# Seven block products for pairs of delta-rule projections, in a four-layer hybrid backbone

## The reference

```python
def streams(h):                     # h: tokens x 1024
    p = h @ w_in                    # q, k: 8 heads x 128; v, z: 16 heads x 128; 64 gate columns
    qkv = silu(centred_dwconv(p[..., :GDN_CONV_DIM], conv_w))     # 4 taps over the tokens
    z = p[..., GDN_CONV_DIM:GDN_CONV_DIM + GDN_VAL_DIM]
    ...                             # q and k to unit length, decays from the gate columns
```

## Time and profile before

| | |
|---|---|
| median of three runs | 3240.86 us |
| the profiled execution: span from first to last instruction | 3251.1 us |
| TensorE busy | 3092.5 us (95%) |
| VectorE, ScalarE, GpSimd busy | 53%, 47%, 27% |
| mean granted clock of TensorE | 0.978 |
| DMA | 261.93 MB, mean 81 GB/s |

### The profile page before, as it was taken

How to read it: one execution, slowest core, us unless ns; L and a number is a source line. 1 busy time by engine, 2 the same in 40 slices (tenths; PEclk the granted TensorE clock), 3 DMA queues, 4 the chain that set the end, 5 groups by cost and what they waited for, 6 DMA issues and landing times. The chain is left out here.

```text
span 3251.1 us, 55663 instructions
## 1 busy us (share of the span) xinstructions
PE 3092.5 (95%) x21673; PEld 2016.4 (62%) x21673; DVE 1731.2 (53%) x3543; ACT 1539.1 (47%) x3296; POOL 873.2 (27%) x652
## 2 busy tenths in 40 slices
PE   5889999999999999999999999897999999999998
PEld 3357777777777764455445555444777777777753
DVE  1156666666666652244443334346676767776632
ACT  3155555555555531256432444335655565555521
POOL 0044434533533410011001101003544435343400
PEclk9699999999999999999999999898999999999999
DMA  9921111211211126022311111102212222121135
GB/s 375 330 68 54 56 56 55 67 56 45 72 56 51 45 89 235 1 68 64 128 33 31 29 46 52 72 4 80 66 53 69 59 60 63 57 68 53 43 120 192
DMA packets 224097, 261.93 MB, mean 81 GB/s; under 512 B 19418, under 2 KB 158948, under 8 KB 223716
## 3 DMA queue, kind: packets, MB, share of 16 engines
q1 hardware_dynamic: 223844, 258.46, 24.7%
HBM read 239.15 MB, written 19.27 MB: 79 GB/s over the span
## 5 line engine op out<-in xcount | busy, mean ns | idle before, releaser
L898 PE MATMUL ps<-hT,W 128*128 128x512 f32 (+1 forms) x2656 | 1001.2, 506 | 3.0 <-DVEq L192 2.0
L898 PEld LDWEIGHTS ps<-hT,W 128*128 128x128 f32 x2656 | 470.5, 193 | 195.1 <-issue 165.6
L1331 DVE CAST_PREDICATED arena<-mask,ps 128x384 bf16<-128x384 uint32 x448 | 253.2, 565 | 223.2 <-PE ps L967 174.3
L1148 ACT CAST arena<-ps 128x384 bf16<-128x384 f32 x384 | 166.9, 482 | 347.7 <-PE ps L954 346.7
L2372 PE MATMUL ps<-arena 128*128 128x512 f32 x712 | 311.2, 595 | 2.3 <-SPq L192 2.0
L1333 DVE CAST_PREDICATED arena<-mask,ps 128x384 bf16<-128x384 uint32 x448 | 250.9, 560 | 0.0
L2372 PEld LDWEIGHTS ps<-arena 128*128 128x128 f32 x712 | 134.5, 191 | 167.1 <-issue 162.8
L2007 PE MATMUL ps<-hT,W 128*128 128x512 f32 (+1 forms) x608 | 218.2, 493 | 0.6 <-DMA W<-in_att_w_in 0.4
L1455 POOL TENSOR_TENSOR arena<-arena 128x768 f32<-128x768 f32 (+1 forms) x32 | 44.4, 1389 | 636.0 <-ACT arena L1192 636.0
L1268 DVE SCALAR_TENSOR_TENSOR arena<-arena,vec 128x770 f32<-128x770 f32 (+1 forms) x192 | 205.4, 1070 | 6.8
L967 PEld LDWEIGHTS ps<-arena 128*128 128x128 bf16 x2304 | 144.7, 98 | 55.4 <-issue 51.0
(11 more groups left out here) (284 smaller groups left out, 6177.0 us busy)
## 6 DMA issues: line engine op xcount, KB each, us to landing
arena<-in_ada_w SPq DMA_DIRECT2D x24, 2048.0 KB, 19.5
W<-in_gdn_w_in SPq DMA_DIRECT2D x95, 512.0 KB, 4.0
arena<-decay_sums SPq DMA_DIRECT2D x64, 384.0 KB, 4.1
W<-decay_rows SPq DMA_DIRECT2D x64, 384.0 KB, 5.0
arena<-in_gdn_w_out SPq DMA_DIRECT2D x32, 512.0 KB, 10.5
W<-in_gdn_w_out SPq DMA_DIRECT2D x30, 512.0 KB, 3.4
arena<-gated SPq DMA_DIRECT2D x32, 384.0 KB, 7.7
gated<-arena SPq DMA_DIRECT2D x24, 384.0 KB, 2.3
```

Of the source, the lines that this page charges most:

```text
L898: mm = pe.matmul(ps[:, b, 0:t1 - t0], w[:, i, :], env.hT[:, i, t0:t1], start=(i == 0), stop=(i == KD - 1))
L1148: act.copy(half_cols(Xb[d], s, d), ps[:, 2 * d, 0:384].rearrange("p (c b s) -> p c b s", c=NT, s=s)).then_inc(*inxe.up(m, lv, d))
L1331: dve.copy_predicated(half_cols(Mb[d], s, d), wide(env.m4[:, d, lv]), src_m).then_inc(*inm.up(m, lv, d, "m"))
```

## The change

The projections of k with q, and of v with z, are formed as a 2 x 2 block product: the two tiles are the two block rows, the contraction is halved (4 matmuls in place of 8), and the tokens are halved (384 each in layer 0, 256 each in layer 3, there of the latent tokens alone). Seven products named 1 to 7 take the place of eight. A1 .. A7 are those of k and q (once per two slots), B1 .. B7 those of v and z (every slot). The first pair of each kind keeps the old form, so that 7 A pairs and 15 B pairs of each layer are changed. In layer 3 the context columns of k and v stay separate (c0, c1).

Some products accumulate on another one that stays in the bank (`CHAIN`) and that ScalarE has copied out meanwhile. All products are copied out by ScalarE, and VectorE adds the parts one position later (`late`). Sums of activations go into the space of `env.x` (GpSimd, once per layer), so x is loaded again from DRAM at the end of slot 14; after layer 2 it is stored for this. The sums of the weights are formed on GpSimd for k and q (`a_sums`, `a_last`) and on VectorE for v and z (`b_sums`, `b_last`). The constants for rotary attention leave the start's load and are loaded ahead of layer 2.

```diff
+CHAIN = {"A6": "A1", "A3": "A5", "A4": "A7", "B6": "B1", "B5": "B6", "B3": "B5", "B4": "B7"}
+def slot_order(n, last):
...
+    elif odd:
+        order = ["A7"] * heads + (["c1"] * fresh if last else o[:1]) + ["A4"] * heads + ["B1"] * fresh + (o if last else o[1:])
+        order += ["B6", "B2", "B5", ("B7", 0, 1), "B3"] * fresh
+    else:
+        if last:
+            order = ["c0", "A5", "A2", "A3"] * heads + o + ["B1", "c1", "B6", "B2", "B5", ("B7", 0, 1), "B3"] * fresh
+        else:
+            order = ["A5", "A2", "A3"] * heads + o[:1] + ["B1"] * fresh + o[1:] + ["B6", "B2", "B5", ("B7", 0, 1), "B3"] * fresh
...
+    spare = [("B7", i, i + 1) for i in range(1, KD2)] * fresh + [("B4", i, i + 1) for i in range(KD2)] * fresh
+    if odd and n + 1 < 2 * GH - 2:
+        spare += [(use, i, i + 1) for use in ("A1", "A6") for i in range(KD2)]
...
+        def strassen(n, use, i, o):
...
+            elif i == 0 and which != 2:
+                form = {6: 2, 5: 1, 3: 4, 7: 3, 4: 3}[which]
+                sig, key = (aform, h) if kind == "A" else (bform, m)
+                pe.wait_ge(sig.sem, sig.at(key, form))
...
+            return pe.matmul(o, w, x, start=(i == 0 and use not in CHAIN), stop=(i == KD2 - 1), ...)
...
-                if p == 14 and m in U:
+                if p == (15 if n >= 0 else 14) and m in U:
                     silu_v(m)
+                if p == 15 and n in U and n:
+                    gates(n)
                 for use in done[n, p] if n > -2 or p >= 2 else []:
                     keep(n, use)
...
                 if p == 7 and n in TILES and n > -2:
-                    conv_x(n)
+                    conv_x(n, True, False)
+                if p == 8 and n in TILES and n > -2:
+                    conv_x(n, False)
...
-                if p == 13 and m in U:
+                if m in U and p == (14 if n >= 0 and step_at(n, "B3") == 13 else 13):
...
+                    conv(1, 16 + m, convv, m, 0, True, p == 14)
...
+                if m in U and m and p == min(3, max(0, first_step(n, "B6") - 2)):
+                    b_sums(m)
+                for key in late[n, p]:
+                    add(*key)
+                    if key[1] == "B2":
+                        b_last(m)
...
+        def a_last(h):
+            kb = env.W[:, 0, KD2:]
+            pool.wait_ge(ad.sem, ad.at(2 * h - 2, "A2"))
+            pool.wait_ge(aform.sem, aform.at(h, 2))
+            pool.tensor_tensor(kb, kb, SUMS["A"][1], ALU.subtract).then_inc(*aform.up(h, 4))
```

More of the change, by code:

```diff
@@ L160, in build @@
         env.ps = ctx.enter_context(nc.psum_tensor("ps", [P, 8, 512], F32))
[L161 to L164, removed]
+        env.ident, env.ones, env.cap_f, env.cap_b, env.perm = (env.cst[:, i * P:(i + 1) * P] for i in range(5))
         env.m4 = env.mask[:].rearrange("p (two l c) -> p two l c", two=2, l=LEVELS)
@@ L547, in fill_plan @@
 def fill_plan(last):
     plan, done, uses, before, last_in = {}, {}, [], {}, {}
-    bank = 6
     for n in range(-2, GU + 1):
-        unit, tile = 0 <= n + 1 < GU, n < 2 * GH - 2
-        fresh = unit and n >= 0
         short = last and n % 2 == 1
[L559 to L587, removed]
-            else:
[L589 to L602, removed]
@@ new lines, in fill_plan, with cost, begin @@
+        order, small, spare = slot_order(n, last)
+        bank, spare_bank, doing = 6, None, None
+        spent, goal, turn = 0.0, 0.0, 0
+        def cost(use):
+            if use[0] in "AB":
+                return (1.0 if last else 1.5,) * KD2
+            return COST[use[0]] if use[0] in COST else COST[use[1]] if use[0] in "XVZ" else ((1,), (2,))[int(use[1])]
+        def begin(use, of_spare):
+            nonlocal bank, spare_bank
+            if use in CHAIN and (n, CHAIN[use]) in before:
+                at = before[n, CHAIN[use]][0]
+            elif of_spare and spare_bank is not None:
+                at = spare_bank
+            elif not of_spare and spare_bank is not None and spare:
+                at = 13 - spare_bank
+            else:
+                at = bank
+            if of_spare:
+                spare_bank = at
+            before[n, use] = (at, last_in.get(at))
+            last_in[at] = (n, use)
+            bank = 13 - at
@@ L603, in fill_plan @@
+        step_of = lambda item: (item[0], item[1], True) if isinstance(item, tuple) else (item, CT if item == "G0" and short else 0, False)
+        total = sum(sum(cost(step_of(i)[0])) if not isinstance(i, tuple) else cost(i[0])[0] for i in order + small + spare if step_of(i)[0][0] != "t")
+        share = max((total - sum(FILL[:2])) / sum(FILL[2:]), 0.5) + 0.001
+        least = (lambda use: FIRST[use]) if n == -2 else (lambda use: AFTER.get(use[0], 0))
         for p in range(POS):
@@ L606, in fill_plan @@
             here = []
[L607 to L611, removed]
+            while spent < goal or n == -2:
+                if doing is None:
+                    if order:
+                        queue = order
+                    elif small and p >= least(small[0]) and (turn == 0 or not spare):
+                        queue = small
+                    elif spare:
+                        queue = spare
+                    else:
+                        break
+                    use, step, single = step_of(queue[0])
+                    if p < least(use):
+                        break
+                    queue.pop(0)
+                    turn = 1 if queue is small else 0
+                    if step == 0 or not single:
+                        begin(use, single)
+                    doing = [use, step, step + 1 if single else len(cost(use))]
+                use, step, stop = doing
+                here.append((use, step, len(cost(use))))
+                spent += cost(use)[step]
+                doing = [use, step + 1, stop] if step + 1 < stop else None
             plan[n, p] = here
@@ L614, in fill_plan @@
             uses += [(n, use) for use in done[n, p]]
-        assert at == len(steps)
+        assert not order + small + spare and doing is None
     return plan, done, uses, before
@@ L1193, in silu_x, with gates @@
                                ACT.Silu).then_inc(*sx.up(n, i))
-            if n == -1 or last and n > -2:
+            if n > -2:
+                hold(env, act)
+                act.preload_act_table_set(LNEXP)
+        def gates(m):
+            act.wait_ge(dev.sem, dev.at(m - 1, "B4"))
+            sz = v.sz[:, m % 2, LO:T]
+            act.activation(sz, sz, ACT.Silu).then_inc(*zsd.up(m))
+            if m == GU - 1:
                 hold(env, act)
@@ L1264, in conv @@
             lo = lo + 2 if lo else 0
[L1265 to L1266 removed]
+            if first:
+                dve.tensor_scalar(acc[:, lo:CONVW], pad[:, lo:CONVW], col(0), None, ALU.mult).then_inc(*sig.up(key, 0))
+            for w in range(1 if first else 2, 4 if second else 2):
                 dve.wait_ge(sig.sem, sig.at(key, w - 1))
@@ L1463, in gpsimd @@
             m = n + 1
+            if n in TILES and n >= 0 and n % 2 == 0:
+                a_last((n + 2) // 2)
             if m in U:
@@ L2336, in out_phase @@
     stored = seq("stored", per(1) if last else [], 16)
+    before_last = l == DEPTH - 2
+    kept = seq("x_kept", [(n,) for n in range(SEQ // P)] if before_last else [], 16)
     def sync(sp):
```

247 lines of the change are left out of this document (212 added, 35 removed).

## The result

The changed kernel takes 3510.1 us (median of 4 runs, 3497.8 to 3516.0), the kernel before on the same chip 3241.5: ratio 1.081, 95% interval 1.079 to 1.084, **268.6 us slower** by the medians, 264 by the ratio. Forecast were 3312 us and +71. The direction was right; the size lies far outside the range of 3210 to 3355.

What follows compares the result with a forecast made beforehand. TensorE's program order was taken as the clock in both layers. Saving -93, waits +175, VectorE +5, convolution split -14 and start -2 summed to +71 us: 3312 us on the median, range 3210 to 3355.

Steps and rivals of the forecast that it cites:

- The saving, -93 us: TensorE's matmul stream: 2.6 us saved a pair in layer 0, 1.65 in layer 3, for 22 pairs each.
- Rival 4: Nothing is multiplied less: a 384-column matmul costs nearly what 512 do; 3444 us, chance 0.02.
- ScalarE's hand-overs and `a_last`: TensorE's waits for bank copies, the norm and GpSimd's subtraction: 76 us in layer 0, 99 in layer 3, together +175.
- Touching products: Successive uses of one bank with nothing between: TensorE waits 0.75 us in layer 0, 0.65 in layer 3.
- B3 at p 9: Layer 3, odd slots: B3 waits 2.7 us for B5's copy, behind `silu_x` and two table loads on ScalarE.
- G1 at p 15: Layer 3, odd slots: G1 directly behind A6 waits 3.3 us for ScalarE's cast, table load, silu, gates and copies.
- G1's and k0's waits in layer 0: Odd slots, positions 15 and 16: G1 waits 0.65 us and k0 1.0 us for copies queued on ScalarE.
- rivals 1 and 2: Smaller waits: 1, only short hand-overs, 3178 us, chance 0.12; 2, waits 90 to 125 us, about 3244 us, 0.15.
- VectorE, 5 us: Added weight sums and additions, +6.1 us a slot in layer 0, +5.0 in layer 3, mostly hidden: 5 us in all.
- Rival 3: VectorE becomes the bound where its share passes 75%, in the inverse's loop: +40 on the forecast, 3350 us, chance 0.16.
- Splitting the convolution (-14): Both convolutions split over two positions, removing most of layer 3's waits behind masked copies: 1 us a slot, -14.
- What would show it: Right: waits for ScalarE's copies, slots of 64 and 60 us. Wrong: layer 0 slots under 62.5 us, or VectorE-ended waits.

Runs made afterwards that it cites:

- x1: Changed kernel with ScalarE's evictions of finished products placed ahead of silu_x, silu_v and the gates in their position, nothing left out: 3508.6 us, ratio 1.080.
- y1: Changed kernel with VectorE's weight sums and late additions and GpSimd's splitting all cut to one column: 3384.9 us, ratio 1.043.
- z2: Kernel before with four added 512-column VectorE additions a slot on scratch memory, three at position 8 and one at 9: 3272.4 us, ratio 1.009.
- y2: Kernel before with four added 512-column VectorE additions a slot on scratch memory, three at position 3 and one at 9: 3320.3 us, ratio 1.022.
- z3: y2 with the four added additions cut to one column each: 3247.0 us, ratio 1.000 to the kernel before.
- y3: y1 with the edit of x1 (evictions ahead of Silu in ScalarE's position): 3373.6 us, ratio 1.039.

## Why the prediction was wrong

**The saving, -93 us: right.** Six records of 384 columns in the changed kernel's layer 0 are one row:

```profile
632.03 2.10 PE L972 MATMUL ps<-hT,W 128*128 128x384 f32 x6
```

Less the last record's own 0.49 us, its five spacings are 0.322 us each, as drawn between the two ends of the earlier trace rows. Rival 4 is out. (By the prediction's own terms layer 3 saves 17.2 - 15.5 = 1.7 us a pair, not 1.65; that makes 1 us.)

**ScalarE's hand-overs and `a_last`: right in place and nearly in size.** A4 behind A7: 1.8 forecast, 2.1 in the list (line 1221). `a_last`: 1.4 against 1.5, 14 times, 21.2 us in all (the operation itself took 1.27 us, not the 1.17 of the earlier trace rows; twice VectorE's 0.685 would be 1.37, where the prediction wrote 1.34). A1 behind B4: 1.75 against 1.5. Touching products: 0.75 against 0.57 in the list and 0.84 in the start times. Layer 3, B3 at p 9: 2.7 against 3.0; G1 at p 15: 3.3 against 2.9; G0 behind the norm: 1.65 against 2.1. Not found were G1's and k0's waits in layer 0. Over two slots 10.85 against 8.0, and 14.15 against 12.0; by 7 that is 140 us for the 175 forecast, so rivals 1 and 2, with waits under 104 and of 90 to 125 us, are out as well. x1 adds that these waits aren't independent of the loop: two of them could be removed for nothing. No run takes the hand-overs away as a whole; their price rests on the lists.

**VectorE, 5 us: the step that failed.** The text counted its instructions (+6.1 and +5.0 us a slot; the terms that it names make 5.8 in layer 0) at durations from rows in which nothing ran beside them, and took the added work as lying in idle time. The lists show 12.0 and 5.6 us of waits for VectorE in two slots beyond the norm's, after 0 and 1.6: by 7 some 112 us. y1 has 126 for VectorE and its neighbour together, clock included: the time lost to the half clock is 122.0 us in the changed kernel, 82.5 in y1 and 72.8 in the kernel before, and that TensorE's fewer waits brought it down is likely, not shown. Two errors lie in the step. First, the sums were put at position 3, in the middle of the 17 us block in which GpSimd splits and caps. The kernel before has that block too, and a sign of the price was in its trace, which I had read past. Beside the 1021 ns for 770 columns of the earlier trace rows stood (2300 to 3050 us):

```profile
L1268 DVE SCALAR_TENSOR_TENSOR arena<-arena,vec 128x512 f32<-128x512 f32 x21 | 24.4, 1161 | 0.7
```

The shorter shape is the slower one: in one slot its four instructions run from 2583.10 us, and GpSimd's capping from 2582.07 to 2585.84. A mean that doesn't grow with the size is a wait inside the instruction. Second, even 2.8 us without a neighbour cost a microsecond a slot (z2): at that place the loop had less room than the "idle gaps" suggest.

The Trainium skill states the rule in SBUF — State Buffer, section "SBUF: two separate sides": a VectorE instruction with two inputs in SBUF, or in a mode that uses both of its ports, and one of GpSimd share a pair of ports under an exclusive lock held for a whole instruction, and the loser blocks. The runs agree: 0.146 us becomes 1.59. In the traces VectorE's operations with an operand in PSUM stay at 0.95 us for 768 columns throughout, as the earlier trace rows' 284 ns for 128 columns do. Which of the two cases holds for the convolution's first instruction no run shows; it reads one tensor and one column of constants, and is held as well (1.42 us at 646.79, with GpSimd's line 1663 until 647.80, against 0.61 alone). I had weighed another rule of the skill, on GpSimd's speed, and not this one, which speaks against the change.

**Rival 3** (VectorE becomes the bound above 75%, 3350 us, chance 0.16) named the right engine. Its busy share did come to 75 and 77%. But the share isn't what decides: y2 has the loss of 73 us with VectorE at 69% in the stretch of layer 0, and z3 none.

**Not in the sum at all.** The account of two slots of layer 0 is 124.5 - 7.8 (saving) + 20.0 - 0.8 (waits listed) = 135.9, measured 143.4; in layer 3, 111.7 - 4.95 + 17.6 - 1.6 = 122.8, measured 131.2. 7.5 and 8.4 us are open, about 111 us in all. A part is the clock. In every second slot of layer 0 there is one stretch of 6.83 us at the lower level. It is the second of these lines, between the time before and after it (columns as in the earlier trace rows; the granted clock is the third number from the end):

```profile
560.30:567.10 6.80, 4.47 (x39) 2.87 (x37) 6.69 (x5) 3.31 (x12) 6.58 (x5) 1.00 0.30 80
567.13:573.96 6.83, 4.64 (x26) 4.04 (x27) 4.16 (x10) 2.72 (x8) 6.67 (x5) 0.50 0.00 0
574.00:581.00 7.00, 7.00 (x59) 4.62 (x58) 4.03 (x8) 4.16 (x10) 1.23 (x1) 1.00 0.00 0
```

The stretch loses 3.4 us. The two slots of layer 3 above have three such stretches of 3.41 us, 5.1 us lost (the pairs after them have two, and take 129.7 us). The kernel before had none in layer 0 after 290 us. Over the program the clock costs about 49 us more than before (122.0 us of full-speed time lost after 72.8). The other part is the 0.27 us that a hand-over costs beyond the list: for 17 and 12 waits more than before, 4.6 and 3.2 us, an estimate from y1's hand-over. Together that is 8.0 and 8.3 us for the 7.5 and 8.4. The first slots of layer 0 also have a wait of 6.7 us for an eviction (line 1203) and one of 3.6 for GpSimd's squares, priced at nothing and absent before.

So by the lists of two slots, times seven, the loss is -89 (saving) + 134 (hand-overs) + 112 (VectorE) + 111 (surplus of the hand-overs, and clock) = 268 us, against the forecast's -93, +175, +5 and nothing, with -14 and -2 beside them. That the hand-overs came out 35 us below the forecast hid a part of the two misses.

**Splitting the convolution (-14), the rest (0), the start (-2).** The gain of the split can't be read apart, since VectorE's waits behind the masked copies grew instead. What lies outside the slots came out 7 us shorter, near the -2 and the noise of one profile.

"What would show it" named a_last's 1.4 us and the waits of about 3 us at p 9 and p 15, which came, and as the sign of being wrong "waits that VectorE ends", which came too: with the norm's they are 19.7 of the 37.6 us in the two lists. Slots of 64 and 60 us are nearly y1's (66 and 62), not the changed kernel's.

## What to carry to other kernels

Before work with its operands in SBUF goes to VectorE or GpSimd, lay its place over the other's timeline, and price it as its own duration plus the rest of the other's running instruction (up to 1.6 us here, whatever the size). Then ask how much room the loop has at that very place: in layer 0, 2.9 us cost nothing and 4.9 cost 2 to 3 us a slot. A block product that saves 2.6 us for a pair of tiles doesn't pay where it adds hand-overs of 0.84 us and more, weight sums and additions of its parts.

## What was not expected of the hardware

- VectorE and GpSimd take turns by whole instructions when both work in SBUF: one column 1.59 us against 0.146; GpSimd's 768 columns 1.97 to 2.10 us against 1.65.
- A wait of TensorE costs more than its length in the list: 0.74 us between starts for 0.57 listed, and 0.10 us more on the records behind it.
- With waits of up to 4.1 us spread over two slots of layer 0, 20 us in all, came a half-clock stretch of 6.8 us, in a stage that had none; in y1's layer 0, with 10 us of waits, none over 2.1 us, mostly one of 3.4 us. Each loses half its length. That the waits are the cause isn't shown: y3 has waits like y1's and loses 73.2 us to the clock over the program, the kernel before 72.8.
